# First two quads of each feed-forward: token sums on VectorE instead of GpSimd, the reciprocal moved behind the first panel's quads, weight rests moved forward

## The reference

```python
def sq_relu_mlp(h, w_up, w_down):
    u = jax.nn.relu(h @ w_up)
    return (u * u) @ w_down

xp = xp + sq_relu_mlp(rms_norm(xp, norm_mlp[i]), mlp_up[i], mlp_down[i])
```

## Time and profile before

| | |
|---|---|
| median of 3 runs | 1825.52 us (1820.56 to 1831.78) |
| the profiled execution | 1825.37 us, of which 1823.6 us from the first to the last instruction |
| mean granted TensorE clock | 0.956 of full |
| busy: TensorE, VectorE, ScalarE, GpSimd | 93%, 62%, 45%, 26% of the span |
| first feed-forward: plain block 0 begins | 346.3 us |
| second feed-forward: plain block 0 begins | 1452.2 us |

### The profile page before, as it was taken

How to read it: one execution, slowest core, us unless ns; L and a number is a source line. 1 busy time by engine, 2 the same in 40 slices (tenths; PEclk the granted TensorE clock), 3 DMA queues, 4 the chain that set the end, 5 groups by cost and what they waited for, 6 DMA issues and landing times.

```text
span 1823.6 us, 33516 instructions
## 1 busy us (share of the span) xinstructions
PE 1689.2 (93%) x13615; PEld 1559.3 (86%) x13615; DVE 1130.1 (62%) x1710; ACT 825.3 (45%) x1371; POOL 466.4 (26%) x384
## 2 busy tenths in 40 slices
PE   7999988999999998999789798897988999999997
PEld 6989767999999997999788797575765999999997
DVE  5070466775767675476776864787623785757673
ACT  4253344352635352333455543677753342626261
POOL 4344234300000003445222221687912210000000
PEclk9999879999999999999999999799998999999999
DMA  4212122321313232331321210001285223222221
GB/s 177 93 47 93 50 99 96 139 75 66 139 47 138 75 115 95 110 123 47 116 105 47 93 59 1 1 2 48 94 341 214 92 70 117 93 93 92 92 92 47
DMA packets 26149, 170.15 MB, mean 93 GB/s; under 512 B 2154, under 2 KB 13978, under 8 KB 16234
## 3 DMA queue, kind: packets, MB, share of 16 engines
q1 hardware_dynamic: 23434, 133.31, 19.6%
q0 software_dynamic: 2592, 35.13, 5.2%
HBM read 156.26 MB, written 12.17 MB: 92 GB/s over the span
## 4 chain that ended last, share of the span: by engine, by line
PE 70%; DVE 15%; ACT 9%; issue 3%; POOL 2%; DMA 0%; ACTq 0%; DVEq 0%; SPq 0%; PEldq 0%
PE slot L2883 19%; PE slot L2650 16%; PE slot L2814 15%; PE slot L3000 3%; PE slot L2619 2%; ACT phase L1706 2%; PE slot L3008 2%; PE slot L2733 2%; POOL phase L1080 1%; PE slot L2978 1%; PE slot L3138 1%; DVE xt_rest L2379 1%; PE slot L3198 1%; PE slot L3109 1%; ACT phase L1720 1%
## 5 line engine op out<-in xcount | busy, mean ns | idle before, releaser
L2814 PE MATMUL slot<-h_high,w_high 128*128 128x260 f32 x784 | 224.1, 286 | 6.9 <-DVE w_rest L2071 5.2
L2814 PE MATMUL slot<-h_high,w_rest 128*128 128x260 f32 x784 | 223.3, 285 | 0.0
L2814 PE MATMUL slot<-h_rest,w_high 128*128 128x260 f32 x784 | 223.1, 285 | 0.0
L2883 PE MATMUL slot<-u_high,w_high 128*128 128x260 f32 x1024 | 206.6, 283 | 0.0
L2883 PE MATMUL slot<-u_rest,w_high 128*128 128x260 f32 x1024 | 205.7, 282 | 0.0
L2883 PE MATMUL slot<-u_high,w_rest 128*128 128x260 f32 x1024 | 205.4, 282 | 0.0
L2883 PEld LDWEIGHTS slot<-u_high,w_rest 128*128 128x128 f32 x1024 | 157.9, 188 | 0.0
L2883 PEld LDWEIGHTS slot<-u_high,w_high 128*128 128x128 f32 x1024 | 157.4, 188 | 0.5
L2883 PEld LDWEIGHTS slot<-u_rest,w_high 128*128 128x128 f32 x1024 | 157.5, 188 | 0.0
L2814 PEld LDWEIGHTS slot<-h_high,w_high 128*128 128x128 f32 x784 | 149.8, 191 | 8.8 <-issue 6.5
L1080 POOL TENSOR_SCALAR phase<-phase 128x128 f32<-128x128 f32 (+3 forms) x128 | 140.2, 1112 | 44.3 <-DVE phase L1816 44.0
(11 more groups left out here) (455 smaller groups left out, 4626.0 us busy)
## 6 DMA issues: line engine op xcount, KB each, us to landing
weights<-in_wt SPq DMA_DIRECT2D x47, 2048.0 KB, 8.0
weights<-in_state SPq DMA_DIRECT2D x2, 2048.0 KB, 9.0
out<-weights SPq DMA_DIRECT2D x2, 2048.0 KB, 8.4
weights<-in_w SPq DMA_DIRECT2D x2, 2048.0 KB, 9.0
out<-phase SPq DMA_DIRECT2D x6, 512.0 KB
x_rows<-residual SPq DMA_DIRECT2D x1, 2080.0 KB, 6.7
residual<-x_rows SPq DMA_DIRECT2D x1, 2080.0 KB, 10.5
phase<-in_x_prompt SPq DMA_DIRECT2D x2, 1024.0 KB, 6.6
```

The lines of the kernel that those rows point to most:

```text
L2814: last = mm(bank, weights[w][:, KH * half + k, :], h_part[m][:, of_h, k, :], start=start and k == 0 and w == 0 and m == 0, stop=k == KH - ...
L2883: last = mm(ps[:, a, 0:HT], w[:, k, :], m[:, k, HT * a:HT * a + HT], start=k == 0 and w is high and m is x_high, stop=k == DC - 1 and w is ...
```

## The change

GpSimd no longer makes the token sums. DVE makes them, between the other instructions of its `first_quads`. The reciprocal moves behind `u_rest(i, 3)` of the first panel. A1's rest moves right behind S12's rest, and T3's rest from the first place among the rests to the last. ACT's order and TensorE's waits follow: TensorE now waits for T3's rest ahead of the product that uses it.

```diff
@@ gpsimd
-            def sums_of_tokens(layer):
-
-                pool.wait_ge(h_rest_ready, 16 * layer + 12)
-                slots = (T1, T1, T3, ALU.subtract), (T3, T3, T2, ALU.subtract), (T2, T2, T1, ALU.add), (T4, T4, T2, ALU.subtract)
-                for n, (out, a, b, op) in enumerate(slots):
-                    if n:
-                        pool.wait_ge(h_sums_ready, 4 * layer + n)
-                    nc.gpsimd.tensor_tensor(h_raw[:, out, :, :], h_raw[:, a, :, :], h_raw[:, b, :, :], op).then_inc(h_sums_ready, 1)
-
-            sums_of_tokens(0)
...
-            sums_of_tokens(1)
@@ scalar, first_quads
                     token_sums_high(T1, 0)
                     token_sums_high(T3, 1)
+                    token_sums_high(T2, 2)
                     plain_relu(1)
                     s12_high(0, 2)
+                    a1_high(0, 2, 0, DC)
                     act.wait_ge(up_added, added_count(layer, 0, ("plain", 1)))
                     u_high(0)
-                    token_sums_high(T2, 2)
-                    a1_high(0, 2, 0, DC)
                     plain_relu(2)
@@ vector
+                def sums_of_tokens(of):
+
+                    for n in of:
+                        out, a, b, op = ((T1, T1, T3, ALU.subtract), (T3, T3, T2, ALU.subtract), (T2, T2, T1, ALU.add),
+                                         (T4, T4, T2, ALU.subtract))[n]
+                        if n:
+                            dve.wait_ge(h_sums_ready, 4 * layer + n)
+                        else:
+                            dve.wait_ge(h_rest_ready, 16 * layer + 12)
+                        nc.vector.tensor_tensor(h_raw[:, out, :, :], h_raw[:, a, :, :], h_raw[:, b, :, :], op)\
+                            .then_inc(h_sums_ready, 1)
+
                 def first_quads():
 
+                    sums_of_tokens((0, 1))
                     squares(0)
+                    sums_of_tokens((2,))
+                    s12_sums(layer, 0, 2)
                     ps, fr = await_product(dve, ("ms", 2 * layer + 1))
                     link(nc.vector.tensor_scalar(halves(rstd_sq), tok(ps), EPS, None, ALU.add))
                     dve.sem_inc(fr, 1)
-                    link(nc.vector.reciprocal(rstd_sq, rstd_sq))
-                    s12_sums(layer, 0, 2)
+                    sums_of_tokens((3,))
                     squares(1)
-                    token_sums_rest(T3, 2, 2)
                     s12_rest(layer, 0, 2)
+                    a1_rest(layer, 0, 2, 0, DC, "A1")
                     u_rest(0, 0)
                     token_sums_rest(T1, 1, 3)
                     squares(2)
                     dve.wait_ge(full[where(("ff", layer), 0, 2)[0]], where(("ff", layer), 0, 2)[1] + 1)
                     s34_sums_of(layer, 0, 2)
                     token_sums_rest(T2, 3, 4)
-                    a1_rest(layer, 0, 2, 0, DC, "A1")
                     s34_rest(layer, 0, 2)
+                    token_sums_rest(T3, 2, 2)
                     squares(3)
@@ vector, panel
                     u_rest(i, 3)
+                    if start:
+                        link(nc.vector.reciprocal(rstd_sq, rstd_sq))
                     down_rest(layer, i, 3)
@@ tensor, quad
                     if first:
-                        pe.wait_ge(h_rest_ready, 16 * layer + 14)
+                        pe.wait_ge(h_rest_ready, 16 * layer + 13)
                     half_product(w, s12, 0, T1, True)
                     if first:
-                        pe.wait_ge(h_rest_ready, 16 * layer + 15)
+                        pe.wait_ge(h_rest_ready, 16 * layer + 14)
                     half_product(v, s12, 1, T2, True).then_inc(up_product_done, 1)
...
+                    if first:
+                        pe.wait_ge(h_rest_ready, 16 * layer + 15)
                     pe.wait_ge(up_added, added_count(layer, i, ("op1", q)))
                     half_product(v, s34, 0, T3, False).then_inc(up_product_done, 1)
```

## The result

Changed kernel: 1816.8 us median of 6 runs (1815.5 to 1819.5), kernel before in the same comparison: 1827.3 us (1820.6 to 1831.8). Ratio 0.9936, 95% interval 0.9918 to 0.9954: **some 0.6% faster**, 8 to 15 us. The profiled execution took 1819.45 us, its span is 1817.5 us, only 6.1 us less than the span of before.

A forecast was written before the change was run, and what follows sets the result against it. TensorE, busy 93% of the span, was taken as the bound, so only its waits could be gained: 4.80 + 6.27 = 11.1 us off the 1825.52 us median gives 1814.4, stated as 1814.5 us; range 1807 to 1822 us.

The forecast's parts named there:

- the two waits: TensorE's feed-forward waits, 5.2 us for A1's rest and 0.9 us for the mean square's slot, would both go.
- the sum as forecast: Closing TensorE's waits returns 4.80 us in the first feed-forward and 6.27 in the second, together 11.1 us.
- DVE's order in steps: DVE's new first-layer schedule: slot freed 1.0 us before due, A1's rest done at 363.2 against 370.3 us.
- the second copy: Inside quad 2, the two copies TensorE waits for end at 373.8 us, due 374.6, 0.8 us to spare.
- the addition behind P6: Inside quad 2, the addition of 0.70 us behind product P6 ends at 375.6 us, due at 376.1.
- The duration taken for a sum: Each token sum on DVE takes 1.23 us, from a token block's rest; best 1.14, worst 3.4 us.
- The readings of the down products: The down-projections' first readings slip by some 3 us; DVE is back in step by the third, at no cost.
- wait for a weight tile: First tile's load ends at 354.1 us, DVE needs it at 355.8; loads and moved waits cost 0 to 1 us a layer.
- GpSimd and DVE in each other's way: DVE's slow stretch beside GpSimd's token sums is mutual hindrance; 6.4 us of slowed DVE work would go.
- rival (a): A shorter wait (T1's high part, copies or late tile) replaces quad 2's gap: 1816.5 to 1818.5 us or 1821; chance 0.17.
- The half clock: TensorE's half-pace matmuls after quad 2's gap cost 1.34 and 2.80 us; closing the gap returns both.
- Rival (b): Half clock is dealt out anew between feed-forwards, 5 us either way: 1809.5 to 1819.5 us; chance beyond 3 us 0.19.

The follow-up runs named there:

- run 7: Changed kernel plus four GpSimd subtractions per layer on constants, written to unused scratch; 359.98 and 359.84 us per feed-forward, ratio 1.0056 to the kernel before.
- run 8: Changed kernel plus twelve GpSimd memsets of scratch, writes only, where the token sums were; 350.83 and 350.76 us per feed-forward, 1813.2 us (one run).
- run 6: Kernel before plus 12 matmuls of zeros ahead of TensorE's wait for A1's rest; 354.33 and 354.34 us per feed-forward, ratio 0.9992 to the kernel before.
- run 12: Kernel before, unchanged, profiled once more; 357.14 and 354.36 us per feed-forward, median 1826.8 us, ratio 0.9988.
- run 10: Changed kernel with the old order of rests (T3's first, A1's behind T2's); 350.78 and 350.81 us per feed-forward, ratio 0.9968 to the kernel before.
- run 1: Kernel before with only the token sums moved to DVE; 352.73 and 352.71 us per feed-forward, ratio 0.9953 to the kernel before.
- run 2: Kernel before with only the reciprocal moved behind the first panel's quads; 352.31 us in each feed-forward, ratio 0.9970 to the kernel before.
- run 3: Kernel before with only A1's high part and rest moved behind S12's; 353.48 and 353.51 us per feed-forward, ratio 0.9970 to the kernel before.
- run 4: Kernel before with the change's order of rests and reciprocal place, sums still on GpSimd; 352.01 and 351.97 us per feed-forward, ratio 0.9957 to the kernel before.
- run 5: Changed kernel with the reciprocal back ahead of the rests; 351.81 and 351.84 us per feed-forward, ratio 0.9968 to the kernel before.
- run 9: Changed kernel plus nine GpSimd copies per layer from constants, one SBUF input; 357.64 and 358.76 us per feed-forward, 1830.5 us (one run).

## Why the prediction was right, and where it was off

**The bound and the two waits.** Right: both waits went, no other took their place, and the feed-forwards gave back 11.1 us, the sum as forecast (4.80 + 6.27, measured 4.79 + 6.35). Both figures take the kernel before from the same profile, so their agreement shows that nothing of the waits is left, and not that the next execution of the kernel before would lose as much. The median moved by 10.5 us, with 8 to 15 us as its interval. The prediction held a change under 1% to be hardly told from none; six runs of each did tell 0.6%.

**DVE's order in steps.** Counted from the first plain matmul, forecast and measured (changed kernel, rows above): the mean square read at 11.5 and 11.45 us, A1's rest at 16.9 and 16.9, the second copy done at 27.5 and 27.2 (due at 28.3), the addition behind P6 at 29.3 and 29.2. The duration taken for a sum, from the nearest row of like size, held to 0.01 us, and the reciprocal takes 3.40 us in both kernels. The readings of the down products were back in step at the fourth, not the third; nothing waited for that. Nor did DVE wait for a weight tile: the S12 sums (358.37 us) and the S34 sums (368.64 us) follow the instructions before them without idle time.

**GpSimd and DVE in each other's way.** Read from one pair of rows, and shown by runs 7 and 8. The Trainium skill ("SBUF — State Buffer", SBUF: two separate sides) says that an SBUF port pair is shared by the two and locked for a whole instruction, by a DVE instruction with two SBUF inputs only against a GpSimd one that reads SBUF. The runs agree on each point they touch: subtractions and copies block (3.3 and 2.0 us for 1.2), fills don't (1.2), and DVE instructions with fewer than two SBUF inputs aren't blocked (last section).

**Which part does what.** The prediction gave the gap to the three parts together and didn't part them. Against an idle-only 354.35 us (runs 6 and 12) the sums alone give 1.6 us a layer, the reciprocal alone 2.0, A1 first alone 0.9; sums and reciprocal together give all 3.5 (run 10), and the new order of rests nothing on top. Each alone is cut short by what is late next, as rival (a) had it; in the full change that rival didn't occur.

**The half clock: the step that was off.** The prediction took 1.34 and 2.80 us as what closing the gaps returns. (It gave the two parts as 6.8 and 4.2 us; its own figures make 6.9 and 4.1.) The idle part is sure, 2 x 3.5 = 7.0 us. The clock's part differs from execution to execution, 0 to 2.8 us for each gap of the same length, 1.7 us in the mean of the four that were seen: 7.0 + 2 x 1.7 = 10.5 us. That the one profile behind the prediction lay near this mean, at 4.1 us of a possible 0 to 5.6, was luck; with the second profile of the kernel before (run 12) the same two differences are 6.31 + 3.55 = 9.9 us. The median's 10.5 us has an interval of 8 to 15 us and can't tell these apart. In runs 1 to 5, where gaps or late copies of 0.2 to 1.7 us stayed, no half clock followed any of the ten.

**Rival (b).** It was right in kind and too small. Where no kernel differs, a stretch moves from one profile to the next: 346.3 to 351.2 us ahead of the first feed-forward in thirteen profiles, 742.4 to 754.1 us between the two in all of them. Between the feed-forwards the granted clock goes with it: 0.96 at 742.4 us, 0.95 where the stretch took 746.3 to 750.6, 0.94 where it took 751.7 to 754.1. The prediction's "5 us either way" is the scatter of one execution, not of the change; the medians average it, and one pair of profiles (6.1 us apart) would have told half the gain.

## What to carry to other kernels

Before moving work to an idle GpSimd, look at what the DVE does meanwhile: if its instructions there have two SBUF inputs and GpSimd's read SBUF, each waits for one of GpSimd's. Here four sums on GpSimd slowed DVE by 6.4 us, and the same four made by DVE itself took it 5.0 us (2.52 + 1.23 + 1.24). When a wait stands behind a list of instructions in order, work out what is late next before picking one to move: the reciprocal, which nobody needed for 40 us, was worth more (2.0 us a layer alone) than A1's rest moved forward (0.9). Where a program's total scatters by more than the gain, measure the stretch between two instructions that enclose the change: here it repeats to 0.1 us where no half clock falls in it, while single executions of the kernel before lay between 1816 and 1834 us.

## What the runs showed of the hardware that was not expected

The same 2.62 us of idle on TensorE was followed by half clock in three cases of four, for 1.3 to 2.8 us of lost time, and by none in the fourth. The four gaps of 1.6 to 1.7 us (runs 1 and 3) were never followed by it, the four of 5.3 and 7.5 us (runs 7 and 9) always, at half pace for 2.9 to 5.3 us. With matmuls of zeros in the gap the pace was full in both feed-forwards. DVE's reciprocal, the first 1.5 us of which lay beside a GpSimd addition, took 3.40 us, as it did without GpSimd; so did its `tensor_scalar` from PSUM, wholly beside it, with 0.69 us. A square, which reads one SBUF tensor as both inputs, went from 0.69 to 2.72 us. And the blocking goes both ways: the same GpSimd copy took 1.05 us alone and 1.93 us beside such DVE instructions.
